# Two gated delta-rule recurrences in a mixed model kernel: the state read through the keys, the transfers of the block inverse merged, and weight loads placed one pair later

## The chip, the cores and the metric

The kernel runs on one core of one Trainium2 chip. The metric is the device time of one execution in microseconds (us). Matrix products run on TensorE (PE in the profile; its weight loads are PEld), elementwise work on VectorE (DVE) and ScalarE (ACT), small serial work on GpSimd (POOL), and SyncE (SP) issues nearly all DMAs. Each engine runs its own instructions in order and the engines meet through semaphores.

## The reference, cut to what matters

The model is three blocks: a gated delta-rule mixer with a mixture of experts (MoE), a state-space mixer with MoE, and a block of an S5 scan, a convolution and sparse attention with a feed-forward layer. The change touches the first mixer alone. For each head, a chunk of the sequence has keys k, queries q, values v, a write strength beta and a cumulative log decay gcum, and a state S of 128x128 is carried from chunk to chunk:

```python
kb = kc * bc[..., None]
lower = jnp.where(strict, jnp.einsum('nbhid,nbhjd->nbhij', kb, kc) * decay, 0.0)
rhs = jnp.concatenate([vc * bc[..., None], kb * jnp.exp(gcum)[..., None]], axis=-1)
sol = lax.linalg.triangular_solve(eye + lower, rhs, left_side=True, lower=True, unit_diagonal=True)
u, w = sol[..., :dv], sol[..., dv:]
...
def step(S, inp):
    v_new = u_i - jnp.einsum('bhck,bhkv->bhcv', w_i, S)
    o = (jnp.einsum('bhck,bhkv->bhcv', q_i * jnp.exp(g_i)[..., None], S)
         + jnp.einsum('bhij,bhjv->bhiv', a_i, v_new))
    S = (S * jnp.exp(g_last)[..., None, None]
         + jnp.einsum('bhck,bhcv->bhkv', k_i * jnp.exp(g_last[..., None] - g_i)[..., None], v_new))
```

With T the inverse of (eye + lower), v_new is T(beta v) - (T(beta exp(gcum) k)) S, and this is also T(beta v - beta exp(gcum) (k S)). The recurrence runs forward and backward over 768 tokens.

## The kernel before, in words

The eight heads are worked in two halves of four heads (`hg` 0 and 1). In each half a projection makes q, k and v, then a recurrence runs, then `gdn_out` makes the output. The recurrence has six pairs (p = 0 to 5, n = 6 hg + p): a pair is one chunk of 128 tokens of the forward direction and one of the backward direction (u = 0 and 1, "units"). One block of work is four heads of one unit: four 128x128x128 products into one bank of PSUM (eight matmul instructions in the trace, two per fp32 product), or one 128x512 instruction on VectorE or ScalarE.

The matrix "lower" of a pair (`rX`) is made two pairs ahead (`decays`, `scores`; the last step counts up `r_xt`). Its inverse begins with its 16x16 diagonal blocks, which take a way through memory:

- SP writes both matrices to `low_in` in HBM (line 887, 2 DMAs of 256 KB, after `r_xt`), waits until they landed, and reads the blocks back with one block to a partition (line 892, 8 DMAs of 8 KB).
- GpSimd inverts all of them (`low_inverse`, lines 993 to 1002), counting up `r_el`.
- SP writes the inverses and their transposes as blocks to `low_u` and `low_t` (line 900, 16 DMAs of 8 KB), waits, and reads the four whole matrices back into `rU` and `rT` (lines 907 and 908, 4 DMAs of 256 KB).
- Only when these landed does the loop go to the next pair. After pair 1 it issues the loads of `EARLY`, six of 1 MB: the weights of the gate and of the output projection and two items of the next stage. In the first pair it issues the loads of `GAP_LATE` between lines 892 and 900.

TensorE's order in a pair is written out by hand: `level_y` (line 1297) waits for the inverted blocks of this pair; then `level_update` (1305, 1306), `decays` and `scores` of pair p + 2, the second level, `last_y` (1317), `last_update` (1329) and between these `turned` (1340, 1341: k and v transposed). Then for both units `weights_w` (1350: T times beta exp(gcum) k, transposed), `values_own` (1357: T times beta v, with a `spread` on line 1260 that broadcasts the decays), `values_state` (1368: minus w S onto the same bank), `output_state` (1376) and `output_own` (1384 the output, 1386 the state's update). Between them stand ScalarE's negated copy of w into `rX` (line 2350, `r_nw`), its Exp of the spread (2353, `r_eb`) and its copy of v_new into `vB` (2356, `r_vnc`). VectorE scales the transposed k into `kB` and v into `vB` (2981 and 2982, `r_kvs`), makes `rY` for the state (2988, `r_yc`), the queries (2994, 2996, `r_q`), and adds to output and state (3002 to 3005, `r_state`) in the next pair.

Of the kernel before, what the change touches and what calls it, by code (L numbers as in the profile page):

```python
# [9 lines left out]
ALU = mybir.AluOpType  # L10
# [363 lines left out]

def build(nc, A):
    with ExitStack() as stack:
# [76 lines left out]
        beg = carve(NT, 16)  # L453
        ea = carve(16)
# [4 lines left out]
        rD, rY, kB, vB, qE = ([carve(HG, P) for _ in range(2)] for _ in range(5))  # L459
# [378 lines left out]
        LOW_DMAS, LOW_BASE = 16 * 30, 16 * 4  # L838

        def blocks_of(name, u, j):  # L840

            whole = A[name][u].rearrange("p j c -> j (p c)" if False else "p j c -> p j c")
            return bass.AP(whole.tensor, whole.offset + j * P, [[LOW * HG * P + LOW, P // LOW], [HG * P, LOW], [1, LOW]])
# [20 lines left out]
        def _(sp):  # L864
# [15 lines left out]
            def low_blocks(hg):  # L880

                for p in range(PAIRS):
                    n = hg * PAIRS + p
                    sp.wait_ge(s.r_low, LOW_DMAS * n + LOW_BASE)
# [8 lines left out]
                    if p == 0:  # L893
                        for item in GAP_LATE[hg]:
                            load(item)
# [5 lines left out]
                    sp.wait_ge(s.r_low, LOW_DMAS * n + 416 + LOW_BASE)  # L901
# [45 lines left out]
        def _(pool):  # L947
# [32 lines left out]
            def low_inverse(n):  # L980
# [4 lines left out]
                if n:  # L985
                    pool.wait_ge(s.r_low, LOW_DMAS * (n - 1) + 416 + LOW_BASE)
# [4 lines left out]
                pool.wait_ge(s.r_low, LOW_DMAS * n + 160 + LOW_BASE)  # L991
# [90 lines left out]
        def _(pe):  # L1082
# [164 lines left out]
            def recurrence(hg):  # L1247
# [96 lines left out]
                def weights_w(p, u):  # L1344

                    n, b, z = hg * PAIRS + p, own(p, u), 2 * (p % 2) + u
                    pe.wait_ge(s.r_kvs, 2 * n + u + 1)
                    pe.wait_ge(s.r_u, 4 * n + 2 + u + 1)
                    for j in range(HG):
                        mm = pe.matmul(ps[:, b, heads[j]], kB[u][:, j, :], rU[z][:, j, :], start=True, stop=True)  # L1350
                    mm.then_inc(s.r_w, 1)

                def values_own(p, u):

                    n, b, z = hg * PAIRS + p, own(p, u), 2 * (p % 2) + u
                    for j in range(HG):
                        pe.matmul(ps[:, b + 1, heads[j]], rU[z][:, j, :], vB[u][:, j, :], start=(j == 0), stop=False)
                    pe.wait_ge(s.r_tbq, n + 1)
                    spread(tbq, u, side(p, u) + 1).then_inc(s.r_in2, 1)

                def values_state(p, u):

                    n, b = hg * PAIRS + p, own(p, u)
                    pe.wait_ge(s.r_nw, 2 * n + u + 1)
                    if p:
                        pe.wait_ge(s.r_state, 2 * (n - 1) + u + 1)
                    for j in range(HG):
                        mm = pe.matmul(ps[:, b + 1, heads[j]], rX[2 * (p % 3) + u][:, j, :], S[u][:, j, :], start=False, stop=(j == HG - 1))
                    mm.then_inc(s.r_vn, 1)
# [33 lines left out]
                for p in range(PAIRS):  # L1403
# [21 lines left out]
                    for u in units:  # L1425
                        weights_w(p, u)
                    for u in units:
                        values_own(p, u)
                    for u in units:
                        values_state(p, u)  # L1430
# [774 lines left out]
        def _(act):  # L2205
# [107 lines left out]
            def recurrence(hg):  # L2313
# [20 lines left out]
                for p in range(PAIRS):  # L2334
# [16 lines left out]
                    for u in units:  # L2351
# [415 lines left out]
        def _(dve):  # L2767
# [80 lines left out]
            def gdn_scalars():  # L2848
# [13 lines left out]
                v.do(dve.tensor_tensor(beg, beg, beta, ALU.mult))  # L2862
# [40 lines left out]
            def recurrence(hg):  # L2903
# [73 lines left out]
                def scaled(p, u):  # L2977
# [3 lines left out]
                    v.do(dve.tensor_tensor(kB[u], g3(side(p, u)), bc(beg[:, tile(p, u), i:i + HG]), ALU.mult))  # L2981
                    v.do(dve.tensor_tensor(vB[u], g3(side(p, u) + 1), bc(beta[:, tile(p, u), i:i + HG]), ALU.mult), s.r_kvs)

# [48 lines left out]
                for p in range(PAIRS):  # L3032
# [31 lines left out]
                    for u in units:  # L3064
                        queries(p, u)
# [794 lines left out]
```

## Time and profile before

| | us |
|---|---|
| median of 3 runs | 4190.58 (4190.25 to 4191.65) |
| the profiled execution | 4194.48 |
| its span in the trace | 4192.4 |
| PE busy | 3823.4 (91%) |
| DVE, ACT, POOL busy | 1825.3, 956.7, 356.4 |
| recurrence of the first half, pairs 0 to 5 | 237.8 to 447.5 |
| recurrence of the second half | 713.6 to 919.8 |
| first waits of PE for the inverted blocks (line 1297), whole span | 27.2, 5 times |

The two recurrences are 416 us, a tenth of the span. How to read it: a busy PE is not yet PE at its peak, so what counts for the recurrences is when each pair begins (its first `level_y`), what PE waited for before it, and which steps lie between two beginnings. PE's granted clock is a share of full speed, 0.50 being 1.2 GHz and 1.00 being 2.4 GHz. In a timeline row, "x16" merges that many neighbouring instructions, and the bracket holds the idle time before them and what ended it.

### The profile page before, as it was taken

The numbers are of one execution on the slowest core, as the hardware profiler recorded it, in microseconds if no ns is written. First come the engines' busy times: TensorE is split into PE (matmuls) and PEld (weight loads), VectorE is DVE, ScalarE is ACT, GpSimd is POOL, SyncE is SP. The second block draws the span as 40 slices with busy tenths as digits, with TensorE's granted clock in tenths as the row PEclk, the third lists the DMA queues.
The fourth block names the chain that finished last, engine by engine and source line by source line (L and its number), as shares of the span: only waits on it lengthen the run. The fifth ranks groups of instructions, "written<-read, shape, count | busy, mean of one in ns | idle before, by whom it ended". The sixth has DMA issues, their size and how long they took to land.

```text
span 4192.4 us, 50922 instructions
## 1 busy us (share of the span) xinstructions
PE 3823.4 (91%) x21420; PEld 2362.6 (56%) x21420; DVE 1825.3 (44%) x2843; ACT 956.7 (23%) x1886; POOL 356.4 (9%) x929
## 2 busy tenths in 40 slices
PE   8989999899999999889998989888888998998999
PEld 4578656875644434677776764222355433446777
DVE  3645445554112212478886540110236467415443
ACT  3421133123211111355654221000124200100000
POOL 0033001210000000000000000000040056100000
PEclk8989999999899999799998999999988999999999
DMA  5232122311498897212101436999921011231331
GB/s 197 86 107 62 51 101 74 112 59 52 176 384 338 340 384 285 73 71 81 61 31 41 126 116 277 421 421 421 341 65 57 26 53 49 75 100 54 108 101 51
DMA packets 278563, 631.30 MB, mean 151 GB/s; under 512 B 63552, under 2 KB 205376, under 8 KB 219456
## 3 DMA queue, kind: packets, MB, share of 16 engines
q1 hardware_dynamic: 275712, 627.40, 40.7%
q8 instruction: 169, 2.77, 0.3%
q10 hardware_dynamic: 2624, 0.66, 0.1%
q14 instruction: 58, 0.48, 0.0%
HBM read 611.75 MB, written 16.25 MB: 150 GB/s over the span
## 4 chain that ended last, share of the span: by engine, by line
PE 68%; DMA 11%; DVE 11%; ACT 3%; issue 3%; SPq 2%; POOL 2%; ACTq 0%; DVEq 0%
PE ps L1867 11%; PE ps L1572 11%; PE ps L1209 6%; PE ps L1918 5%; PE ps L1578 4%; DMA arena<-moe_w_down 4%; DMA arena<-moe_w_gate 2%; PE ps L1479 2%; PE ps L2091 2%; PE ps L1457 2%; PE ps L1725 2%; PE ps L1721 2%; PE ps L1730 2%; DMA arena<-moe_w_up 2%; DVE arena L3453 2%
## 5 line engine op out<-in xcount | busy, mean ns | idle before, releaser
L1572 PE MATMUL ps<-arena 128*64 128x512 f32 x3072 | 709.0, 601 | 79.3 <-DMA arena<-moe_w_up 22.4
L1572 PEld LDWEIGHTS ps<-arena 128*64 128x64 f32 x3072 | 207.6, 137 | 528.9 <-issue 385.7
L3191 DVE SCALAR_TENSOR_TENSOR arena<-arena,ps 128x512 f32<-128x512 f32 (+1 forms) x48 | 30.2, 657 | 525.9 <-PE ps L1572 525.9
L1209 PE MATMUL ps<-arena 128*128 128x512 f32 (+1 forms) x768 | 253.9, 489 | 3.5 <-DVE g_rows L2859 2.1
L1918 PE MATMUL ps<-arena 128*128 128x512 f32 x512 | 229.6, 605 | 5.0 <-DVE arena L3453 4.3
L3453 DVE TENSOR_TENSOR arena<-arena,ps 128x512 f32<-128x512 f32 x86 | 58.4, 687 | 370.8 <-ACT arena L2746 143.5
L1725 PE MATMUL ps<-h_first,w_rest 128*128 128x512 f32 (+1 forms) x576 | 214.5, 388 | 0.5 <-DVE arena L3352 0.5
L1209 PEld LDWEIGHTS ps<-arena 128*128 128x128 f32 x768 | 145.9, 191 | 105.8 <-issue 93.6
L3199 DVE TENSOR_TENSOR m_yx_rest<-ps,m_yx_lead 64x512 fp32r<-64x512 f32 x64 | 44.0, 688 | 362.2 <-ACT m_yc_lead L2460 205.7
L1721 PE MATMUL ps<-h_second,w_rest 128*128 128x512 f32 (+1 forms) x576 | 199.8, 362 | 0.4 <-DVE h_second L3257 0.4
L2460 ACT ACTIVATE m_yx_lead<-ps 64x512 fp32r<-64x512 f32 x64 | 37.9, 592 | 660.7 <-PE ps L1572 660.0
L1578 PE MATMUL ps<-arena 128*32 128x256 f32 x3072 | 175.7, 380 | 0.0
L1918 PEld LDWEIGHTS ps<-arena 128*128 128x128 f32 x512 | 98.9, 195 | 134.4 <-issue 127.1
L1867 PE MATMUL ps<-h_lead,w_lead 128*128 128x512 f32 x352 | 139.6, 397 | 11.4 <-DVE h_rest L3391 6.8
L1578 PEld LDWEIGHTS ps<-arena 128*32 128x32 f32 x3072 | 94.7, 109 | 96.8 <-issue 39.0
L1867 PE MATMUL ps<-h_rest,w_lead 128*128 128x512 f32 x352 | 139.5, 396 | 0.0
L1867 PE MATMUL ps<-h_lead,w_rest 128*128 128x512 f32 x352 | 139.1, 395 | 0.0
L1016 POOL IOTA arena<- 128x64 f32 x2 | 0.4, 186 | 1545.3 <-DVE arena L3431 1410.0
L3453 DVE TENSOR_TENSOR arena<-arena 128x512 f32<-128x512 f32 (+4 forms) x181 | 126.5, 739 | 6.2 <-ACT arena L2697 2.6
L1725 PEld LDWEIGHTS ps<-h_first,w_rest 128*128 128x128 f32 x576 | 112.6, 196 | 20.7 <-issue 3.5
L1730 PE MATMUL ps<-h_first,w_rest 128*128 128x512 f32 (+1 forms) x576 | 124.0, 357 | 0.0
L1721 PEld LDWEIGHTS ps<-h_second,w_rest 128*128 128x128 f32 x576 | 111.5, 194 | 20.1 <-issue 3.1
(499 smaller groups left out, 7060.8 us busy)
## 6 DMA issues: line engine op xcount, KB each, us to landing
arena<-moe_w_gate SPq DMA_DIRECT2D x128, 1024.0 KB, 9.0
arena<-moe_w_up SPq DMA_DIRECT2D x128, 1024.0 KB, 10.2
arena<-moe_w_down SPq DMA_DIRECT2D x128, 1024.0 KB, 11.7
arena<-ada_w SPq DMA_DIRECT2D x48, 1024.0 KB, 4.9
arena<-ffn_w_gate_up SPq DMA_DIRECT2D x22, 1024.0 KB, 5.0
arena<-gdn_w_in SPq DMA_DIRECT2D x16, 1024.0 KB, 9.7
arena<-w_in SPq DMA_DIRECT2D x30, 512.0 KB, 3.8
arena<-ssd_w_x SPq DMA_DIRECT2D x8, 1024.0 KB, 5.1
```

Source lines behind the costliest of these rows:

```text
L1209: mm = pe.matmul(ps[:, 2 * (i % 2) + j, 0:nn], state.w[:, k, m * P:(m + 1) * P], hT[:, k, c0:c0 + nn], start=(k == 0), stop=(k == KD - 1))
L1457: mm = pe.matmul(ps[:, 2 + b + 2 * (j % 2), 0:nn], state.w[:, k, (j % 2) * P:(j % 2) * P + P], hT[:, k, c0:c0 + nn], start=(k == 0), stop= ...
L1479: mm = pe.matmul(ps[:, b + 2 * (m % 2), 0:nn], w[j // 2][:, j % 2, m * P:(m + 1) * P], oT[:, j, c0:c0 + nn], start=(j == 0), stop=(j == HG ...
L1572: mm = pe.matmul(ps[CAPX * h:CAPX * h + CAPX, bank, :], x[:, 0:CAPX], w[:, 512 * h:512 * h + 512], **flags)
L1578: mm = pe.matmul(ps[CAPC * q:CAPC * q + CAPC, bank, 0:CW], x[:, CAPX:SLOTS], w[:, CW * q:CW * q + CW], **flags)
L1721: rests = lambda k: pe.matmul(out, wh[:, k, cols_], hT_lo[k][:, x], start=False, stop=(tail_last and k == KD - 1))
L1725: pe.matmul(out, wh[:, k, cols_], hT_hi[k][:, x], start=(k == 0), stop=False)
L1730: mm = pe.matmul(out, wl[:, k, cols_], hT_hi[k][:, x], start=False, stop=(not tail_last and k == KD - 1))
L1867: mm = pe.matmul(out, a[:, k, cols_], tile_of(b, k), start=(k == 0 and n == 0), stop=(k == tiles - 1 and n == 2))
L1918: mm = pe.matmul(ps[:, bank, :], w[:, k, i * P:(i + 1) * P], h2[:, k, :], start=(k == 0), stop=(k == KD - 1))
L2091: mm = pe.matmul(ps[:, (3 * i + x) % 5, :], w[:, k, (i % 2) * P:(i % 2 + 1) * P], h2[:, k, :], start=(k == 0), stop=(k == KD - 1))
L3453: v.do(dve.tensor_tensor(out, a_, b_, op), sem)
```

## The change

- v_new is made in the other order. `key_states` takes the place of `weights_w`: it multiplies k (not transposed) with S. VectorE's `less_state` takes beta exp(gcum) times that from `vB` (four instructions of 128x128 for each unit, with a column of the new `nbeg` = -beta exp(gcum) as scalar). `values` then applies T once. `values_own`, `values_state`, the scaled keys `kB` and ScalarE's negated copy go. `scaled_last` moves behind `queries`.
- In SP's loop the four DMAs back of pair n no longer wait for their landing before the two of the next matrix are issued (they still do in a half's first and last pair), and `level_y` of the pairs 1 to 4 waits until the next pair's matrix has landed as well (`LOW_AT["matrix", n + 1]`).
- The loads of `EARLY` are issued in pair 2, between its blocks and its inverses, and no longer after the DMAs back of pair 1.

```diff
+LOW_PARTS = {"matrix": 2, "blocks": 8, "inverted": 16, "back": 4}
...
+        LOW_AT, landed = {}, 16 * 4
+        for hg in range(GH // HG):
+            for step in low_order(hg * PAIRS):
+                landed += 16 * LOW_PARTS[step[0]]
+                LOW_AT[step] = landed
...
+                def matrix(n):
                     for u in range(2):
                         sp.wait_ge(s.r_xt, 2 * n + u + 1)
-                        sp.dma_start(A["low_in"][u], rX[2 * (p % 3) + u]).then_inc(s.r_low, 16)
-                    sp.wait_ge(s.r_low, LOW_DMAS * n + 32 + LOW_BASE)
+                        sp.dma_start(A["low_in"][u], rX[2 * ((n - first) % 3) + u]).then_inc(s.r_low, 16)
+                    sp.wait_ge(s.r_low, LOW_AT["matrix", n])
...
-                    if p == 1:
+                    if p == 0 or p == PAIRS - 1:
+                        sp.wait_ge(s.r_low, LOW_AT["back", n])
+
+                for n in range(first, first + PAIRS):
+                    matrix(n)
+                    blocks(n)
+                    if n == first:
+                        for item in GAP_LATE[hg]:
+                            load(item)
+                    if n == first + 2:
                         for item in EARLY[hg]:
                             load(item)
+                    inverted(n)
+                    sp.wait_ge(s.r_low, LOW_AT["inverted", n])
+                    back(n)
...
                     if x == 0:
-                        pe.wait_ge(s.r_low, LOW_DMAS * (n + 1) + LOW_BASE)
+                        pe.wait_ge(s.r_low, LOW_AT["back", n] if p in (0, PAIRS - 1) else LOW_AT["matrix", n + 1])
...
-                def weights_w(p, u):
-
-                    n, b, z = hg * PAIRS + p, own(p, u), 2 * (p % 2) + u
-                    pe.wait_ge(s.r_kvs, 2 * n + u + 1)
+                def key_states(p, u):
+
+                    n, b = hg * PAIRS + p, own(p, u)
                     pe.wait_ge(s.r_u, 4 * n + 2 + u + 1)
...
+                    for j in range(HG):
+                        mm = pe.matmul(ps[:, b + 1, heads[j]], k_[:, j, chunk(p, u)], S[u][:, j, :], start=True, stop=True)
+                    mm.then_inc(s.r_w, 1)
+                    pe.wait_ge(s.r_tbq, n + 1)
+                    pe.wait_ge(s.r_kvs, 2 * n + u + 1)
+                    spread(tbq, u, side(p, u) + 1).then_inc(s.r_in2, 1)
+
+                def values(p, u):
+
+                    n, b, z = hg * PAIRS + p, own(p, u), 2 * (p % 2) + u
+                    pe.wait_ge(s.r_nw, 2 * n + u + 1)
+                    for j in range(HG):
+                        mm = pe.matmul(ps[:, b + 1, heads[j]], rU[z][:, j, :], vB[u][:, j, :], start=True, stop=True)
                     mm.then_inc(s.r_vn, 1)
...
-                        act.wait_ge(s.r_w, 2 * n + u + 1)
-                        a.do(act.activation(flat(rX[2 * (p % 3) + u]), ps[:, own(p, u), :], ACT.Copy, scale=-1.0), s.r_nw)
...
+                def less_state(p, u):
+
+                    n, i = hg * PAIRS + p, 8 * u + hg * HG
+                    dve.wait_ge(s.r_w, 2 * n + u + 1)
+                    for j in range(HG):
+                        v.do(dve.scalar_tensor_tensor(out=vB[u][:, j, :], in0=ps[:, own(p, u) + 1, j * P:(j + 1) * P],
+                                                      scalar=nbeg[:, tile(p, u), i + j:i + j + 1], in1=vB[u][:, j, :], op0=ALU.mult, op1=ALU.add),
+                             s.r_nw if j == HG - 1 else None)
...
                     for u in units:
                         scaled(p, u)
+                    v.settle()
+                    for u in units:
+                        less_state(p, u)
+                    for u in units:
+                        queries(p, u)
                     for u in units:
                         scaled_last(p, u)
-                    for u in units:
-                        queries(p, u)
```

## Rows read from the trace of the kernel before

**Rows 1.** Windows of pairs 1 and 2, first half, and pair 2, second; columns on top.
```profile
core 0: us, PE busy (x) PEld busy (x) DVE busy (x) ACT busy (x) POOL busy (x), PEclk, DMA share, GB/s
277.30:310.60 33.30, 32.30 (x281) 29.45 (x279) 20.33 (x40) 7.54 (x18) 11.02 (x32) 1.00 0.34 111
310.60:355.40 44.80, 34.43 (x279) 31.69 (x279) 20.17 (x40) 7.56 (x18) 11.35 (x36) 0.89 0.26 77
...
782.80:827.30 44.50, 33.66 (x279) 30.89 (x279) 20.20 (x40) 7.55 (x18) 11.35 (x36) 0.88 0.27 78
```

**Rows 2.** PE's timeline, where pairs begin: start, length, line, [idle before <- releaser].
```profile
277.38 1.95 PE L1297 MATMUL ps<-arena 128*128 128x128 f32 x16
...
320.03 3.78 PE L1297 MATMUL ps<-arena 128*128 128x128 f32 x16 [9.38 <-DMA arena<-low_t]
...
388.52 1.95 PE L1297 MATMUL ps<-arena 128*128 128x128 f32 x16
...
417.93 1.95 PE L1297 MATMUL ps<-arena 128*128 128x128 f32 x16
...
749.59 1.95 PE L1297 MATMUL ps<-arena 128*128 128x128 f32 x16
...
792.70 3.47 PE L1297 MATMUL ps<-arena 128*128 128x128 f32 x16 [9.84 <-DMA arena<-low_t]
...
890.25 2.05 PE L1297 MATMUL ps<-arena 128*128 128x128 f32 x16 [0.23 <-DMA arena<-low_t]
```

**Rows 3.** Windows of 1 us, engine PE: window, busy, PEclk, DMA share, GB/s.
```profile
314.00:315.00 1.00, 0.00 (x0) 0.71 0.05 6
...
324.00:325.00 1.00, 1.00 (x8) 0.67 0.25 23
```

**Rows 4.** PE's timeline, second part of pair 1 of the first half.
```profile
297.77 1.06 PE L1350 MATMUL ps<-arena 128*128 128x128 f32 x8
299.32 1.16 PE L1350 MATMUL ps<-arena 128*128 128x128 f32 x8 [0.48 <-DVE arena L2982]
...
303.24 2.05 PE L1368 MATMUL ps<-arena 128*128 128x128 f32 x16
...
309.60 1.06 PE L1386 MATMUL ps<-arena 128*128 128x128 f32 x8
```

**Rows 5.** Groups by shape, DVE and ACT: busy us, mean ns of one, idle before.
```profile
L3222 DVE SCALAR_TENSOR_TENSOR arena<-ps,arena 128x512 f32<-128x512 f32 x64 | 47.8, 746 | 10.8 <-PE ps L1662 10.8
...
L2974 DVE SCALAR_TENSOR_TENSOR arena<-ps,arena 128x256 f32<-128x256 f32 x48 | 22.9, 478 | 0.0
...
L2353 ACT ACTIVATE arena<-ps 128x512 f32<-128x512 f32 x8 | 4.8, 597 | 6.5 <-PE ps L1260 6.5
```

**Rows 6.** SP's timeline, first half: back of pair 1, EARLY, matrix and blocks of pair 2.
```profile
263.86 0.34 SPq L907 DMA_DIRECT2D arena<-low_u  x1
...
265.67 1.36 SPq L878 DMA_DIRECT2D arena<-gdn_w_in  x2
...
274.02 8.10 SPq L887 DMA_DIRECT2D low_in<-arena  x2
288.63 4.20 SPq L892 DMA_DIRECT2D arena<-low_in  x8
```

**Rows 7.** SP's timeline, first half: one whole round, back of pair 3 to pair 4.
```profile
345.99 0.34 SPq L907 DMA_DIRECT2D arena<-low_u  x1
...
352.41 0.80 SPq L887 DMA_DIRECT2D low_in<-arena  x2
355.10 2.85 SPq L892 DMA_DIRECT2D arena<-low_in  x8
371.39 0.26 SPq L900 DMA_DIRECT2D low_u<-arena  x1
...
378.42 0.34 SPq L907 DMA_DIRECT2D arena<-low_u  x1
```

**Rows 8.** SP's timeline, second half: first DMA back of pair 1.
```profile
739.14 0.34 SPq L907 DMA_DIRECT2D arena<-low_u  x1
```

More of the change, by code:

```diff
@@ L371, in __init__, with low_order @@
         self.n, self.uses, self.w = 0, [0] * (RING + DEEP), None
+LOW_PARTS = {"matrix": 2, "blocks": 8, "inverted": 16, "back": 4}
+def low_order(first):
+    return [(kind, n) for n in range(first, first + PAIRS) for kind in ("matrix", "blocks", "inverted", "back")]
 def build(nc, A):
@@ L453, in build @@
         beg = carve(NT, 16)
+        nbeg = carve(NT, 16)
         ea = carve(16)
@@ L458, in build @@
         rT, rU = [carve(HG, P) for _ in range(4)], [carve(HG, P) for _ in range(4)]
-        rD, rY, kB, vB, qE = ([carve(HG, P) for _ in range(2)] for _ in range(5))
+        rD, rY, vB, qE = ([carve(HG, P) for _ in range(2)] for _ in range(4))
         low = [carve(LOW * LOW) for _ in range(4)]
@@ L837, in build @@
         EARLY = [PLAN[PLAN.index(FIRST_OUT[hg]):PLAN.index(RECUR_AT[hg])] for hg in range(GH // HG)]
-        LOW_DMAS, LOW_BASE = 16 * 30, 16 * 4
+        LOW_AT, landed = {}, 16 * 4
[3 more added lines that the diff above has]
+                LOW_AT[step] = landed
         def blocks_of(name, u, j):
-            whole = A[name][u].rearrange("p j c -> j (p c)" if False else "p j c -> p j c")
+            whole = A[name][u]
             return bass.AP(whole.tensor, whole.offset + j * P, [[LOW * HG * P + LOW, P // LOW], [HG * P, LOW], [1, LOW]])
@@ L880, in low_blocks, with blocks @@
             def low_blocks(hg):
-                for p in range(PAIRS):
-                    n = hg * PAIRS + p
-                    sp.wait_ge(s.r_low, LOW_DMAS * n + LOW_BASE)
+                first = hg * PAIRS
+                def matrix(n):
                     for u in range(2):
                         sp.wait_ge(s.r_xt, 2 * n + u + 1)
-                        sp.dma_start(A["low_in"][u], rX[2 * (p % 3) + u]).then_inc(s.r_low, 16)
-                    sp.wait_ge(s.r_low, LOW_DMAS * n + 32 + LOW_BASE)
+                        sp.dma_start(A["low_in"][u], rX[2 * ((n - first) % 3) + u]).then_inc(s.r_low, 16)
+                    sp.wait_ge(s.r_low, LOW_AT["matrix", n])
+                def blocks(n):
                     for u in range(2):
@@ L892, in low_blocks, with inverted @@
                             sp.dma_start((low[0], low[1])[u][32 * u + 8 * j:32 * u + 8 * j + 8, :].rearrange("b (r c) -> b r c", c=LOW), src).then_inc(s.r_low, 16)
-                    if p == 0:
-                        for item in GAP_LATE[hg]:
-                            load(item)
+                def inverted(n):
                     sp.wait_ge(s.r_el, n + 1)
@@ L900, in low_blocks, with back @@
                                 sp.dma_start(blocks_of(name, u, j), low[2 + (x + u) % 2][32 * u + 8 * j:32 * u + 8 * j + 8, :].rearrange("b (r c) -> b r c", c=LOW)).then_inc(s.r_low, 16)
-                    sp.wait_ge(s.r_low, LOW_DMAS * n + 416 + LOW_BASE)
+                def back(n):
+                    p = n - first
                     if p == 0:
@@ L985, in low_inverse @@
                 if n:
[L986 removed]
+                    pool.wait_ge(s.r_low, LOW_AT["inverted", n - 1])
                 g.settle()
@@ L990, in low_inverse @@
                 g.do(pool.affine_select(out=w, in_=w, compare_op=ALU.not_equal, fill=1.0, base=0, pattern=[[1, LOW], [-1, LOW]], channel_multiplier=0))
-                pool.wait_ge(s.r_low, LOW_DMAS * n + 160 + LOW_BASE)
+                pool.wait_ge(s.r_low, LOW_AT["blocks", n])
                 g.settle()
@@ L1342, in turned @@
                     mm.then_inc(s.r_kv, 1)
-                def weights_w(p, u):
-                    n, b, z = hg * PAIRS + p, own(p, u), 2 * (p % 2) + u
-                    pe.wait_ge(s.r_kvs, 2 * n + u + 1)
+                def key_states(p, u):
+                    n, b = hg * PAIRS + p, own(p, u)
                     pe.wait_ge(s.r_u, 4 * n + 2 + u + 1)
[L1349 to L1364, printed above, removed]
                     if p:
                         pe.wait_ge(s.r_state, 2 * (n - 1) + u + 1)
+                    else:
+                        pe.wait_ge(s.r_kvs, 2 * n + u + 1)
                     for j in range(HG):
-                        mm = pe.matmul(ps[:, b + 1, heads[j]], rX[2 * (p % 3) + u][:, j, :], S[u][:, j, :], start=False, stop=(j == HG - 1))
+                        mm = pe.matmul(ps[:, b + 1, heads[j]], k_[:, j, chunk(p, u)], S[u][:, j, :], start=True, stop=True)
+                    mm.then_inc(s.r_w, 1)
+                    pe.wait_ge(s.r_tbq, n + 1)
+                    pe.wait_ge(s.r_kvs, 2 * n + u + 1)
+                    spread(tbq, u, side(p, u) + 1).then_inc(s.r_in2, 1)
[4 more added lines that the diff above has]
+                        mm = pe.matmul(ps[:, b + 1, heads[j]], rU[z][:, j, :], vB[u][:, j, :], start=True, stop=True)
                     mm.then_inc(s.r_vn, 1)
@@ L1425, in recurrence @@
                     for u in units:
-                        weights_w(p, u)
+                        key_states(p, u)
                     for u in units:
-                        values_own(p, u)
-                    for u in units:
-                        values_state(p, u)
+                        values(p, u)
                     for u in units:
@@ L2348, in recurrence @@
                     for u in units:
-                        act.wait_ge(s.r_w, 2 * n + u + 1)
-                        a.do(act.activation(flat(rX[2 * (p % 3) + u]), ps[:, own(p, u), :], ACT.Copy, scale=-1.0), s.r_nw)
-                    for u in units:
                         act.wait_ge(s.r_in2, 2 * n + u + 1)
@@ L2861, in gdn_scalars @@
                 dve.wait_ge(s.tl_act, 2)
-                v.do(dve.tensor_tensor(beg, beg, beta, ALU.mult))
+                v.do(dve.scalar_tensor_tensor(out=nbeg, in0=beg, scalar=-1.0, in1=beta, op0=ALU.mult, op1=ALU.mult))
             def project(hg, first):
@@ L3061, in recurrence @@
                         scaled(p, u)
+                    v.settle()
[3 more added lines that the diff above has]
+                        queries(p, u)
                     for u in units:
                         scaled_last(p, u)
-                    for u in units:
-                        queries(p, u)
                 for u in units:
```

1 line of the change is left out of this document (removed).

## Prediction, made before the changed kernel was run

> **What bounds the kernel now.** I read the page first: PE is busy for 91% of the span, so a change inside the recurrences counts only by what it takes off PE's own row of work or off PE's waits. Then I cut the recurrences into windows from one pair's first `level_y` to the next. The reader is to see in [rows 1] that pair 1 of the first half is PE work nearly from end to end (32.30 of 33.30 us), while pair 2 takes 44.80 us for the same 279 matmuls, at a mean clock of 0.89. PE's timeline says why [rows 2]: before pair 2 it stood for 9.38 us, in the second half for 9.84 us, both times ended by a DMA of `low_t`, the last step of the inverse's way through memory. Pair 1 had no such wait, and the last pair of the second half had 0.23 us. So two things limit a half: PE's own work, 33.1 us in each of the pairs 0 to 3 (277.38 to 310.5 [rows 2, 4]) and 29.4 us in the last two (388.52 to 417.93 [rows 2]), and a round of SP, DMA and GpSimd that takes 32.4 us a pair (345.99 to 378.42 [rows 7]). They are nearly even: the 0.23 us is the proof. The forecast therefore follows both through the pairs.
>
> **The 9.4 us wait.** In pair 1, SP issued the DMAs back at 263.86, the six loads of `EARLY` from 265.67, and then the next matrix at 274.02. That issue took 8.10 us, and the matrix had landed only at 288.63 [rows 6]. Loads and matrix, 6.5 MB, thus kept the DMA engines for 23.0 us. An undisturbed round has 9.1 us from the first DMA back to the first block read (345.99 to 355.10 [rows 7]); here it was 24.8 us. The change issues the matrix right after the DMAs back and puts the loads behind the block reads, where GpSimd works anyway.
>
> What it takes away beside the idle time is a slow start: the clock fell from 1.00 to 0.50 within the window 314 to 315, some 4 us after PE had stopped, and came back within 324 to 325, PE having worked from 320.03 [rows 2, 3]. Pair 2 took 44.8 - 9.4 = 35.4 us of its own against 33.1, so 2.3 us in the first half. In the second, 44.5 - 9.8 - 33.1 = 1.6 us [rows 1, 2]. Sum of wait and clock: 11.7 and 11.4 us.
>
> **PE's own work.** From 303.24 to 309.60 PE ran seven blocks, 0.91 us each; the pair ends one block later, at 310.5 [rows 4]. Before, the part from `weights_w` on has twelve blocks and two spreads: 310.5 - 297.77 = 12.7 us. After, ten blocks and the same spreads: two blocks less, 1.8 us. The second `weights_w` also began 1.55 us after the first, 0.64 us more than a block, since it waited for VectorE's scaling of k and v of unit 1 [rows 4]. `key_states` needs neither; its spread does need `vB`, but VectorE then scales one tile instead of two for each unit and is done a whole instruction earlier. So 0.6 us go too. Together 2.4 us a pair, and 14.4 a half.
>
> What must be hidden for that is the new link key_states, `less_state`, `values`. The trace has no 128x128 instruction of that kind. A 512-wide one takes 746 ns, a 256-wide one 478 [rows 5]: by the slope 344 ns for 128 columns. Four cost between 1.07 us (starts 0.27 apart, if they overlap as the slope suggests) and 1.4 us (one after the other). I take 1.15. With key_states(0) at 0: it ends at 0.9, VectorE takes off the state until 2.2, PE meanwhile does spread(0), key_states(1) and spread(1) until 2.9 to 3.0, and values(0) finds its tile. Unit 1: key_states ends about 2.5, VectorE until 3.7, values(1) would start at 3.8: just in time. Then VectorE does both queries, 0.9 us each, until 4.6 and 5.5 (ScalarE's Exp takes 0.60 [rows 5] and begins right after each spread), and PE's output_state wants them at 4.7 and 5.6. `scaled_last` comes after, until 6.1 and 6.7; output_own wants it at 6.5 and 7.4. Margins of 0.1 to 0.4 us: no stall at 1.15 us, about 0.3 us a pair at 1.4. ScalarE loses two copies of 0.60 us a pair, off the path: worth nothing. VectorE trades two scalings for eight short instructions, with 13 of 33 us idle in the pair [rows 1]. Moving `scaled_last` behind the queries is costed at nothing, its cover being output_state; without it, up to 0.6 us a pair.
>
> VectorE's short instructions pay a fixed part: from the two widths, 0.21 of the 0.344 us [rows 5]. The Trainium skill speaks against such splitting (VectorE: DVE Perf Modes, The TRN2 errata: "many small tiles pay it per-tile", tiles of at least 512 are advised). By its table for a PSUM source, 120 cycles plus one per column at 0.96 GHz, four would be an estimated 1.03 us and the margins above would hold.
>
> **The round through memory.** Now SP's own rhythm. From the first DMA back to the first block read it took 6.4 us (1 MB back) plus 2.7 us (the matrix); then 16.3 us to the first inverse written (block reads, GpSimd), then 7.0 us to the next DMAs back: 32.4 us [rows 7]. After, six DMAs of 256 KB stand in the queue together. The 9.1 us can become 6.4 at best (the matrix hidden in the way back) and 9.1 at worst (they only share the bandwidth). I take 7.2, nearer to the low end, since waiting for a landing has a part in which nothing moves; the round is then 30.5 us, between 29.7 and 32.4.
>
> But PE now waits for matrix and back in the pairs 1 to 4, not for back alone. Followed through the first half: back of pair 1 is issued at 263.86, all six have landed at 271.1, block reads are issued until 273.9, then the 6 MB of loads, which at the pace above occupy the queue for 21 us, until 295. The inverses of pair 2 are ready at 271.1 + 16.3 = 287.4 and would be through at 294.4, but they stand behind the loads: 296. Then landed and ready for PE: 303.2, 333.7, 364.2 for the pairs 2 to 4, and for the last pair, which waits for back alone, 387.5 + 6.4 = 393.9. PE would come to them at 305.7 (275.0 plus 30.7), 336.4, 367.1 and 394.1. So PE never waits, by 0.2 to 2.9 us, and the half ends 26.1 us earlier (11.7 + 14.4). Pair 0's wait stays, as its order is untouched.
>
> In the second half the way back of pair 1 starts at 739.14 for a pair that begins at 749.59, 10.45 us, against 13.52 in the first half [rows 2, 6, 8]: 3.1 us less in hand. There the pairs 2 to 4 are even to within 0.6 us and the last pair waits some 2.9 us: 11.4 + 14.4 - 2.9 = 22.9 us.
>
> **Sum.** 26.1 + 22.9 = 49.0 us. Everything after a recurrence starts from its last matmul (`gdn_out`'s loads have long landed even one pair later: pair 3 begins near 336, they are wanted near 421), so it moves as a whole. The profiled execution would go from 4194.5 to 4145.5. It stands 3.9 us above the median of the runs, 4190.58, and I set the forecast against the median: 4141.5 us. Ends of the unknown prices: with a round of 29.7 us nothing waits, 52 us gained, and with 0.3 us more a pair from VectorE's side 4138; a PE gain of 2.7 instead of 2.4 us a pair, which the round then mostly eats, 4136.
>
> **Rivals.**
> 1. *The round sets the pace.* If the six DMAs only share the bandwidth (9.1 us, a round of 32.4 us), the last pairs wait 7.5 us in the first half and 10.6 in the second, and each wait beyond some 4 us costs about 2 us of clock [rows 3]. Gain 52 - 18 - 4 = 30 us, 4160. A smaller form: the sixteen small writes of pair 2 can't even be issued while the loads fill the queue, as the matrix's two took 8.10 us [rows 6]. Then they go out after 295, the DMAs back follow at about 302 instead of 296, and both halves lose some 6 us: 37 us, 4153. For it: the 8.10 us, and the evenness of round and PE. Against it: the 13.4 us from the last block read's issue to the first inverse (357.95 to 371.39 [rows 7]) cover more than half of the loads. The Trainium skill says the same of the queue (DMA: Bandwidth & Descriptors, Queues, rings and completion order): descriptors on each engine are taken in ring order. The landing at 288.63 agrees, and no sum here needs the sentence.
> 2. *VectorE's link stalls PE.* If the short instructions cost so much, with the semaphores between, that PE loses what the two blocks gave, only waits and clock are won: 23 us, 4167. For it: margins of 0.1 us at three places. Against: the slope of [rows 5].
> 3. *Slower than before.* The same link, but so long that it eats everything: from key_states(1) to the last `scaled_last` VectorE is now one serial queue on which values, output_state and output_own of both units hang. It decides from 2.4 + 23/12 = 4.3 us of stall a pair. If each 128-wide instruction cost the full 746 ns, the link would be 3 us longer than planned, still 1.3 short of it; at 5 us a pair, the kernel would take about 4199. Nothing in the rows has that price.
> 4. *It does not do what it says.* The wait before pair 2 is moved, not removed: PE's new wait for matrix n + 1 is late by as much, because `r_xt` comes late. But that matrix is ready two pairs ahead. Gain then 12 times 2.4 less what the round eats, 15 to 20 us: 4173.
>
> **Chances.** Forecast, 4135 to 4148: 0.60. Rival 1 with both forms, 4148 to 4161: 0.22. Rival 2: 0.08. Rival 4: 0.03. Rival 3: 0.03. Within 0.2% (8.4 us, about what a measurement of this kernel can tell from no change): 0.02. The rest, 0.02, for more gain than 56 us. The range of 4134 to 4160 takes in the forecast and rival 1. Faster by over 0.2%: 0.95; within: 0.02; slower: 0.03.
>
> **What would show it.** In the changed kernel: no idle time before pair 2's `level_y` and a clock of 1.00 from pair 1 on; pair lengths on PE of 30.7 and 27.0 us; in SP's timeline about 7.2 us from the first DMA back to the first block read; the first inverse of pair 2 written near 287 and its DMAs back near 296; PE idle on VectorE before `values`, `output_state` and `output_own` of at most 0.3 us a pair in all; a short wait for a DMA before the last pair of the second half. The forecast is wrong if the pairs are longer than 31.5 us with PE waiting for VectorE (rival 2), or if waits for DMAs stand before several of the pairs 2 to 5 (rival 1), or if what follows the recurrences does not move with them.

## The result and the profile after

| | before | after |
|---|---|---|
| median, us | 4191.11 (4 runs) | 4153.77 (4151.91 to 4156.37, 4 runs) |
| span of the profiled execution | 4192.4 | 4153.3 |
| recurrence of the first half, first `level_y` to last matmul | 209.6 | 190.7 |
| recurrence of the second half | 206.2 | 185.9 |

The ratio is 0.9909, with a 95% interval from 0.9895 to 0.9923: 37 us faster, where 49 were forecast. The two recurrences are 39.1 us shorter, and so is the span: all of the gain lies in them. Since the rest of the program varies by some microseconds from run to run, the recurrences' lengths in the trace are the finer instrument below. They have a limit of their own, told under the experiments.

Where pairs begin in the changed kernel, on PE's timeline (start, length, line, in brackets the idle time before and its releaser; `level_y` is now line 1326):

```profile
274.07 1.95 PE L1326 MATMUL ps<-arena 128*128 128x128 f32 x16
...
305.10 2.05 PE L1326 MATMUL ps<-arena 128*128 128x128 f32 x16 [0.28 <-DMA low_in<-arena]
...
337.28 2.05 PE L1326 MATMUL ps<-arena 128*128 128x128 f32 x16 [1.24 <-DMA low_in<-arena]
...
369.02 2.05 PE L1326 MATMUL ps<-arena 128*128 128x128 f32 x16 [0.64 <-DMA low_in<-arena]
...
399.07 3.68 PE L1326 MATMUL ps<-arena 128*128 128x128 f32 x16 [2.81 <-DMA arena<-low_t]
...
761.60 2.05 PE L1326 MATMUL ps<-arena 128*128 128x128 f32 x16 [1.59 <-DMA low_in<-arena]
...
852.95 3.65 PE L1326 MATMUL ps<-arena 128*128 128x128 f32 x16 [2.94 <-DMA arena<-low_t]
```

They answer to [rows 2]. The two waits of 9.4 and 9.8 us are gone, but waits on a DMA now stand before six of the eight pairs 2 to 5, where before, beside pair 2, only one of 0.2 us stood. `low_in` as releaser is the new thing: PE waits for the next pair's matrix. The last pair of each half begins slowly (3.68 us for sixteen matmuls that take 1.95). Windows on engine PE show that this is the clock (window, its length, busy time and count, PEclk, DMA share, GB/s):

```profile
398.00:399.00 1.00, 0.00 (x0) 1.00 0.04 14
399.00:401.00 2.00, 1.93 (x9) 0.54 0.00 0
401.00:402.00 1.00, 1.00 (x7) 0.50 0.00 0
402.00:403.00 1.00, 1.00 (x8) 0.72 0.00 0
403.00:404.00 1.00, 1.00 (x11) 1.00 0.00 0
```

After the wait of 2.81 us the granted clock was near 0.50 for some 3 us.

The second part of pair 1 on PE, to be laid beside [rows 4] (1382 `key_states`, 1393 `values`, 1401 `output_state`, 1411 the state's update):

```profile
294.47 1.05 PE L1382 MATMUL ps<-arena 128*128 128x128 f32 x8
...
295.87 1.16 PE L1382 MATMUL ps<-arena 128*128 128x128 f32 x8
...
297.38 2.05 PE L1393 MATMUL ps<-arena 128*128 128x128 f32 x16
299.27 1.98 PE L1401 MATMUL ps<-arena 128*128 128x128 f32 x16
...
303.77 1.06 PE L1411 MATMUL ps<-arena 128*128 128x128 f32 x8
```

No bracket stands in it: PE waits for nothing there. From `key_states` to the pair's end at 304.66 (its last block's start plus 0.9 us, as in the prediction) it takes 10.2 us, where it took 12.7. VectorE's side of the same stretch, and its new instruction in the view by shape:

```profile
295.63 1.13 DVE L3008 SCALAR_TENSOR_TENSOR arena<-ps,arena 128x128 f32<-128x128 f32 x4 [0.27 <-PE ps L1382]
297.07 1.13 DVE L3008 SCALAR_TENSOR_TENSOR arena<-ps,arena 128x128 f32<-128x128 f32 x4 [0.31 <-PE ps L1382]
298.11 0.16 DVE L3022 COPY arena<-arena 128x4 f32<-128x4 f32 x1
298.31 0.84 DVE L3024 TENSOR_TENSOR arena<-arena 128x512 f32<-128x512 f32 x1
```
```profile
L3008 DVE SCALAR_TENSOR_TENSOR arena<-ps,arena 128x128 f32<-128x128 f32 x96 | 27.1, 344 | 6.9 <-PE ps L1382 6.9
```

Four of them take 1.13 us, one 344 ns. Lines 3022 and 3024 are the queries, which begin as soon as unit 1 is done.

SP's timeline of the first half, to be laid beside [rows 6] and [rows 7] (901 matrix, 908 block reads, 891 the loads, 915 inverses, 924 the way back):

```profile
262.71 0.34 SPq L924 DMA_DIRECT2D arena<-low_u  x1
...
264.52 0.91 SPq L901 DMA_DIRECT2D low_in<-arena  x2
270.88 2.84 SPq L908 DMA_DIRECT2D arena<-low_in  x8
273.76 1.91 SPq L891 DMA_DIRECT2D arena<-gdn_w_in  x2
275.72 1.35 SPq L891 DMA_DIRECT2D arena<-gdn_w_out  x2
277.12 7.54 SPq L891 DMA_DIRECT2D arena<-gdn_w_in  x2
287.49 0.42 SPq L915 DMA_DIRECT2D low_u<-arena  x1
...
288.70 0.71 SPq L915 DMA_DIRECT2D low_u<-arena  x1
...
293.54 0.32 SPq L915 DMA_DIRECT2D low_u<-arena  x1
...
296.13 0.33 SPq L915 DMA_DIRECT2D low_t<-arena  x1
297.65 0.35 SPq L924 DMA_DIRECT2D arena<-low_u  x1
...
305.08 4.13 SPq L908 DMA_DIRECT2D arena<-low_in  x8
322.48 0.26 SPq L915 DMA_DIRECT2D low_u<-arena  x1
...
329.52 0.34 SPq L924 DMA_DIRECT2D arena<-low_u  x1
```

The matrix of pair 2 now goes out at 264.52 and has landed at 270.88; before it was 288.63. The loads sit behind its block reads. From the first inverse written to the first DMA back it takes 10.2 us in pair 2 (287.49 to 297.65), against 7.0 in pair 3 (322.48 to 329.52). The difference lies in SP's issues: the first eight of the sixteen writes go out over 6.05 us (287.49 to 293.54), some 0.75 us apart, the others 0.37 us apart as in pair 3, and from the last write's issue to the first DMA back it is 1.5 us in both pairs. So the loads ahead hold up the issuing of the small writes. A round, first DMA back to first DMA back, is 31.9 us here (297.65 to 329.52).

### The profile page after: what moved, and what is told of

It reads as the page before. It is cut to its first block, busy times and chain, and to the rows that moved or that the text cites. A ratio compares the mean times of both kernels' runs of the same rounds, so it can differ in the third digit from the quotient of the medians.

```text
span 4153.3 us, 50594 instructions
## 1 busy us (share of the span) xinstructions
PE 3793.5 (91%) x21228; PEld 2334.8 (56%) x21228; DVE 1836.4 (44%) x2915; ACT 942.2 (23%) x1862; POOL 356.8 (9%) x929
## 4 chain that ended last, share of the span: by engine, by line
PE 66%; DMA 11%; DVE 11%; ACT 3%; POOL 3%; issue 3%; SPq 3%; ACTq 0%; DVEq 0%
PE ps L1595 11%; PE ps L1890 11%; PE ps L1238 6%; PE ps L1941 5%; PE ps L1601 4%; DMA arena<-moe_w_down 4%; DMA arena<-moe_w_gate 2%; PE ps L1502 2%; PE ps L2114 2%; PE ps L1480 2%; PE ps L1748 2%; PE ps L1744 2%; PE ps L1753 2%; DMA arena<-moe_w_up 2%; DVE arena L3484 2%
## 6 DMA issues: line engine op xcount, KB each, us to landing
arena<-moe_w_up SPq DMA_DIRECT2D x128, 1024.0 KB, 10.2
```

## The experiments

The table collects them. Each ratio is against the kernel before on the same chip; "recurrences" is the sum of both halves in the profiled execution, and "pair 0" the part of it from the first `level_y` to the end of pair 0, in both halves together.

| kernel | ratio to before (95%) | recurrences, us | of these, pair 0 |
|---|---|---|---|
| before | 1 | 415.7 | 75.6 |
| after | 0.9909 (0.9895 to 0.9923) | 376.6 | 70.8 |
| x1_early_back | 0.9983 (0.9974 to 0.9992) | 401.8 | 72.8 |
| x2_no_merge | 0.9932 (0.9911 to 0.9952) | 386.8 | 69.7 |
| x3_algebra_only | 1.0011 (1.0000 to 1.0022) | 421.1 | 70.3 |
| x8_algebra_exact | 1.0008 (0.9997 to 1.0020) | 414.5 | 74.2 |
| x4_transfers_only | 0.9950 (0.9930 to 0.9969) | 391.7 | 75.3 |
| x5_spread | 0.9904 (0.9885 to 0.9923) | 376.7 | 71.0 |
| x6_own_semaphore | 0.9913 (0.9897 to 0.9930) | 379.8 | 72.9 |
| x7_half_writes | 0.9870 (0.9855 to 0.9885) | 358.7 | 66.5 |
| x9_half_and_spread | 0.9846 (0.9829 to 0.9862) | 357.4 | 66.5 |
| x10_old_algebra_half | 0.9932 (0.9916 to 0.9949) | 389.6 | 71.6 |

Each length comes from one execution. Pair 0 begins after a wait for DMAs, at a granted clock that differs from trace to trace, and its length follows that clock: with the new algebra 33.7 us in the changed kernel's second half (mean clock 0.94), 35.8 us in the first half of x6_own_semaphore (0.87), 37.2 us in the changed kernel's first half (0.84). So two kernels can differ by some 3 us a half in pair 0 without the edit having a part in it, and where it matters pairs 1 to 5 are given apart. The whole times agree with the lengths on what is large: by the ratios x1 is 31 us slower than the changed kernel, x2 10 and x4 17, by the lengths 25, 10 and 15.

The theory from the profile after: PE's own work is now shorter than the round through SP, DMA and GpSimd, and the round sets when the later pairs begin. The rival: PE's own work still sets the end, and the missing gain is elsewhere.

**The new algebra alone.** The first try kept SP's loop of the changed kernel with its pieces put back (and PE waits for `LOW_AT["back", n]` in every pair):

```diff
-                    if p == 0 or p == PAIRS - 1:
-                        sp.wait_ge(s.r_low, LOW_AT["back", n])
+                    sp.wait_ge(s.r_low, LOW_AT["back", n])
...
                     back(n)
+                    if n == first + 1:
+                        for item in EARLY[hg]:
+                            load(item)
```

> The state read through the keys and the inverse applied once, with SP's order and waits as in the kernel before. Theory (the round sets the end): PE saves 2.5 us a pair on its own work, but the wait before pair 2 grows from 9.4 to about 14 us, and the last pairs begin when their DMAs land. Gain 5 to 10 us, 4181 to 4186. Rival (PE's work is the bound): gain 12 x 2.5 = 30 us, 4161.

It came out 5.4 us longer in the recurrences, not 5 to 10 us shorter. Part of that is the edit: here the loads stand behind the wait for the landing, where the kernel before has them ahead of it, so that they and the matrix of pair 2 go out later (first load in the second half 5.75 us after the first DMA back, against 1.8 us; first block read of pair 2 28.5 and 27.2 us after it, against 24.8 and 24.0). So the same was done with SP's loop copied from the kernel before:

> The state read through the keys and the inverse applied once, with SP's loop and all its waits word for word those of the kernel before (the loads right behind the DMAs back, ahead of the wait for their landing). Theory (the round sets the end): PE's own work falls by 2.5 us a pair, the wait before pair 2 grows by 5 us to about 14.5, the last pair waits 4 to 6 us; recurrences 3 to 8 us shorter than before, 4183 to 4188. Rival (PE's own work is the bound): 25 to 30 us shorter.

PE's timeline of this kernel, pair 2 and the last pair of the first half (`level_y` is line 1306):

```profile
319.68 3.78 PE L1306 MATMUL ps<-arena 128*128 128x128 f32 x16 [13.81 <-DMA arena<-low_t]
...
415.70 3.78 PE L1306 MATMUL ps<-arena 128*128 128x128 f32 x16 [4.67 <-DMA arena<-low_t]
```

Pair 2 begins at 319.68, in the kernel before at 320.03 [rows 2]: PE was ready 4.8 us earlier and waited 4.4 us more. The recurrences are 1.2 us shorter, under the 3 to 8 expected, and the time can't be told from before; pairs 1 to 5 take 340.4 us, in the kernel before 340.1, so in them nothing is gained. PE's pair 1 takes 30.6 us, as in the changed kernel, so PE does save 2.5 us a pair, and all of it behind pair 0 goes into waits (of 13.8, 0.3 and 4.7 us in the first half) and the slow clock after them. The rival, 25 to 30 us, is out.

**The transfers alone.** TensorE, VectorE and ScalarE as before, with the changed kernel's `low_blocks`, `LOW_AT` and waits. Against the changed kernel it reads, in short:

```diff
-                        key_states(p, u)
+                        weights_w(p, u)
                     for u in units:
-                        values(p, u)
+                        values_own(p, u)
+                    for u in units:
+                        values_state(p, u)
```

> SP's new order (matrix with the way back, loads one pair later) with TensorE, VectorE and ScalarE as in the kernel before. Theory: pair 2's wait of 9.4 and 9.8 us and the slow clock after it (2.3 and 1.6 us) go, PE's pairs stay 33.1 and 29.4 us, longer than the round, so hardly a wait is left: gain 20 to 24 us, 4167 to 4171. The two halves of the change then sum to about 30 us where both together gave 37. Rival (the wait moves on to later pairs): gain under 12 us.

The recurrences are 24.0 us shorter (20 to 24 were expected; the median of 4172.5 lies 1.5 us beyond 4167 to 4171), and no pair behind pair 0 waits for anything. Pair 2 (`level_y` is line 1325):

```profile
311.26 1.95 PE L1325 MATMUL ps<-arena 128*128 128x128 f32 x16
```

So the transfers alone give 24.0, the algebra alone 1.2, both 39.1 us: together 13.9 more than their sum. The algebra's 30 us of PE work can be collected only as far as the round allows.

**The place of the loads.**

```diff
-                    if n == first + 2:
-                        for item in EARLY[hg]:
-                            load(item)
                     inverted(n)
                     sp.wait_ge(s.r_low, LOW_AT["inverted", n])
                     back(n)
+                    if n == first + 1:
+                        for item in EARLY[hg]:
+                            load(item)
```

> The changed kernel, but with the six weight loads issued again right after the DMAs back of pair 1, ahead of the matrix of pair 2. Theory (waits and round set the end, PE's own work is covered by them): the matrix lands near 288 us, so the wait before pair 2 is back at 10 to 14 us and the clock falls again; after it the round through memory (31.5 us) is longer than PE's 30.6 us, so nothing is caught up. Gain over the kernel before 7 to 13 us, 4178 to 4184. Rival (the loads' place hardly matters, PE's shorter work carries the gain): within 5 us of the changed kernel, about 4155.

The recurrences are 25.2 us longer than in the changed kernel: the loads' place is the largest part of the change. The time, 4184.9, lies just beyond the 4178 to 4184 expected. The wait is back, but before pair 1 and not before pair 2, since in this kernel pair 1 waits for the matrix of pair 2:

```profile
289.88 3.78 PE L1326 MATMUL ps<-arena 128*128 128x128 f32 x16 [14.89 <-DMA low_in<-arena]
```

**The matrix with the way back.** The change to SP is the first hunk of x3; PE waits for `LOW_AT["back", n]` in every pair.

> The changed kernel, but SP waits for the four DMAs back of every pair before it issues the next matrix, and PE waits for back alone. Theory A (six DMAs together save about 1.2 us a round over 9.1 us, and the round sets the end): the last pairs of both halves begin 2 to 4 us later than in the changed kernel, while the waits of 0.3 to 1.6 us before the pairs 2 to 4 mostly go: 3 to 8 us slower than the changed kernel, 4157 to 4162. Theory B (merging gives nothing, since PE must now wait for the matrix too): same as or faster than the changed kernel, 4150 to 4155.

Theory A held, at more than its upper end: 10.2 us longer. Six rounds average 32.3 us, against 31.4 in the changed kernel, and the last pairs wait 5.8 and 4.3 us. What did not come is that the waits before the pairs 2 to 4 mostly go: one of 3.0 us stands in the first half, 1.4, 0.2 and 2.1 us in the second. Each wait over 2 us also begins its pair at a lower clock.

**PE's wait for both.** The matrix's DMAs count on a semaphore of their own:

```diff
-                        pe.wait_ge(s.r_low, LOW_AT["back", n] if p in (0, PAIRS - 1) else LOW_AT["matrix", n + 1])
+                        pe.wait_ge(s.r_low, LOW_AT["back", n])
```

> The changed kernel, but the matrix DMAs count on a semaphore of their own, and PE waits in every pair for back alone, not for the next matrix too. Theory (the round sets the end): the waits of 0.3 to 1.6 us before the pairs 2 to 4 go, and the wait before the last pair grows by as much; the recurrences keep their length within 2 us. Rival (PE's wait for both DMAs is what costs): recurrences 4 to 5 us shorter, with the last pair's wait unchanged at 3 us.

PE's timeline, pairs 4 and 5 of the first half:

```profile
365.06 2.05 PE L1327 MATMUL ps<-arena 128*128 128x128 f32 x16 [1.40 <-DMA arena<-low_t]
...
396.82 3.78 PE L1327 MATMUL ps<-arena 128*128 128x128 f32 x16 [4.57 <-DMA arena<-low_t]
```

The waits of the middle pairs went for the most part to the last pair, as the theory says. The sum is 3.2 us longer than in the changed kernel, more than the 2 us allowed, but 2.1 of them lie in pair 0, which the edit does not touch; pairs 1 to 5 are 1.1 us longer. The rival wanted 4 to 5 us less and is out. The `low_in` brackets of the changed kernel named a wait that cost nothing of its own that these traces can tell.

**The loads spread.**

```diff
-                    if n == first + 2:
-                        for item in EARLY[hg]:
+                    if 2 <= n - first < 5:
+                        for item in EARLY[hg][2 * (n - first) - 4:2 * (n - first) - 2]:
                             load(item)
```

> The changed kernel with the six weight loads spread, two in each of the pairs 2, 3 and 4, at the same place between block reads and inverses. Theory (the loads delay pair 2's small writes by 3 us, and this delay stands before every later pair, as the round is the slower of the two): pair 2's DMAs back go out 7.0 us after the first inverse instead of 10, the waits before the pairs 2 to 5 fall from 5.6 and 4.9 us a half to 2 to 3 us, and the slow clock of the last pair goes. Recurrences 5 to 9 us shorter than in the changed kernel. Rival (two loads a pair delay each pair's small transfers a little): no shorter.

This missed: 376.7 us, no shorter than 376.6. The first step came as expected, pair 2's DMAs back follow its first inverse by 7.0 us and no longer by 10.2. But the six DMAs behind them then took 7.8, 8.9 and 9.7 us from the first DMA back to the first block read in the first half, and 8.7, 7.8 and 7.6 in the second, against 6.8 to 7.7 in the changed kernel from pair 2 on. Whether this comes from two loads a pair or is the scatter of such DMAs is not settled. Scatter of that size needs no spread loads: with all six in pair 2, x6 has a value of 9.0 us and x10_old_algebra_half one of 9.5.

**A shorter round.** In the last kernels the inverse and its transpose lie interleaved, on chip and in HBM, and one DMA takes both:

```diff
-                            for x, name in enumerate(("low_u", "low_t")):
-                                sp.dma_start(blocks_of(name, u, j), low[2 + (x + u) % 2][32 * u + 8 * j:32 * u + 8 * j + 8, :].rearrange("b (r c) -> b r c", c=LOW)).then_inc(s.r_low, 16)
+                            sp.dma_start(blocks_of("low_ut", u, j), low_both[32 * u + 8 * j:32 * u + 8 * j + 8, :].rearrange("b (r c) -> b r c", c=LOW)).then_inc(s.r_low, 16)
...
-                a, raw, w, wt = (block(x, both) for x in low)
+                a, raw = (block(x, both) for x in low)
+                w, wt = (low_both[both, :].rearrange("p (r s c) -> p r s c", s=2, c=LOW)[:, :, x, :] for x in range(2))
```

> The changed kernel with the sixteen writes of inverted blocks made eight: the inverse and its transpose lie interleaved on chip and in HBM, so one DMA of 16 KB takes both. SP's issue of them takes 3 us instead of 5.9. Theory (the round sets the end): a round falls from 31.4 to 28.5 us, under PE's 30.6; all waits from pair 3 on go, and with them the slow clock of the last pair; recurrences 9 to 13 us shorter than in the changed kernel. Rival (PE or the loads set the end): under 3 us.

SP's timeline, one round, and windows of pair 2 and of the last pair of the first half (window, its length, busy time and count of PE, PEld, DVE, ACT, POOL, then PEclk, DMA share, GB/s):

```profile
342.55 3.15 SPq L917 DMA_DIRECT2D low_ut<-arena  x8
347.25 0.34 SPq L926 DMA_DIRECT2D arena<-low_ut  x1
...
349.06 0.90 SPq L904 DMA_DIRECT2D low_in<-arena  x2
354.43 2.85 SPq L911 DMA_DIRECT2D arena<-low_in  x8
371.29 3.14 SPq L917 DMA_DIRECT2D low_ut<-arena  x8
376.05 0.34 SPq L926 DMA_DIRECT2D arena<-low_ut  x1
```
```profile
297.70:328.30 30.60, 30.01 (x264) 27.51 (x263) 21.11 (x46) 6.35 (x16) 10.49 (x34) 1.00 0.24 60
...
385.90:412.70 26.80, 24.69 (x228) 23.13 (x227) 16.32 (x37) 3.90 (x8) 0.00 (x0) 1.00 0.00 1
```

From the first inverse to the first DMA back it takes 4.7 us, the round 28.8 us (347.25 to 376.05; 28.9 on average), and PE's pairs stand back to back at full clock: one wait of 0.5 us is left behind pair 0. The recurrences are 17.9 us shorter than in the changed kernel, more than the 9 to 13 expected: 13.6 us in pairs 1 to 5 and 4.3 in pair 0. The wait before pair 0 is no part of the recurrences, but with earlier DMAs back it is 1.4 and 1.7 us where it was 4.1 and 4.4, and the mean clock of pair 0 is 0.90 and 1.00 where it was 0.84 and 0.94. That the shorter wait made the clock is likely (x9 has the same waits and the same 66.5 us), but no run tests it by itself. The kernel is 1.3% faster than the one before.

**The bound after that.** Two kernels ask whether PE is now the limit. The first is x7 with the edit of x5, the second x4 with the edit of x7.

> Eight writes of 16 KB instead of sixteen of 8 KB, and the six weight loads spread over the pairs 2 to 4. With eight writes alone one wait was left, 0.7 us before pair 2 of the second half, and in neither half did the last pairs wait. Theory (PE's own work is now the bound): recurrences as long as with eight writes alone, 358 to 360 us, within 3 us. Rival (spreading helps further): 3 us or more shorter.

> TensorE, VectorE and ScalarE as in the kernel before, with SP's new order and eight writes of 16 KB. Theory (the kernel before's work on PE, 33.1 us a pair, is longer than the round with sixteen writes already): shortening the round gives only what pair 0 gains by its earlier DMAs back, about 6 us; recurrences 385 to 390 us against 391.7 with sixteen writes and against 358.7 with the new algebra, so that the new algebra is worth its full 12 x 2.5 = 30 us once the round is short, where it was worth 15 us with sixteen writes. Rival (the new algebra's gain is capped elsewhere): recurrences within 20 us of 358.7.

Both came as the theory has them. With the loads spread as well, 357.4 us, within 3 us of 358.7 (its whole time is the lowest measured, 4127 against 4192 on its chip, but 19 us of its span against x7's lie outside the recurrences and are no effect of this edit that the trace shows). With the old algebra and the short round, 389.6 us. So the new algebra is worth 1.2 us with SP's old loop, 15.1 with the changed one (391.7 to 376.6) and 30.9 with the short round (389.6 to 358.7), and that last is its 12 x 2.54 us of PE work in full. In pairs 1 to 5 alone the three are 0, 10.6 and 25.8 us.

## Why the prediction came out as it did

The sign was right, and so was the account of what the change removes; the size was 12 us too large. The measured 4153.8 lies in the range of 4134 to 4160, but not in the forecast itself (4135 to 4148, chance 0.60): it lies in the interval of rival 1 (4148 to 4161, 0.22), and rival 1's sign, waits for DMAs before several of the pairs 2 to 5, came up. So the range held because it took in rival 1, and the round is the slower chain, as that rival has it. That the rival's smaller form names the very number, 37 us and 4153, is luck: it put some 6 us a half on pair 2's small writes alone, and the shortfall has three sources. By its steps:

- *The 9.4 us wait goes, and the slow clock with it.* Right: 0.28 and 1.59 us of idle time before pair 2, and its own length is 30.8 us. x1 shows that it was the loads' place.
- *PE's own work falls by 2.4 us a pair.* Right: pair 1 takes 30.6 us (274.07 to 304.66), 2.5 less; pair 4 takes 27.1 (369.02 to 396.09) where 27.0 was said.
- *VectorE's link hides.* Right, and the slope between two widths gave the price exactly: 344 ns, four in 1.13 us (taken: 1.15). The lower bound of 1.07 was a slip: it counts four spacings of 0.27 us, where three spacings and the last instruction's 0.344 make 1.15; and no row shows the 0.27, which this trace puts at 0.26. No idle time of PE on VectorE in this part. The Trainium skill's warning against short instructions (VectorE: DVE Perf Modes, The TRN2 errata) is true of their price, 0.21 of 0.344 us fixed, and the 1.03 us that the prediction worked out from its table for four was 0.10 low; but they lie in a stretch where PE had other work. Rivals 2 and 3 had no part in it.
- *The way through memory becomes 30.5 us a round.* This term was mis-sized: rounds took 31.9, 31.9 and 31.4 us in the first half, 30.3, 30.4 and 32.7 in the second, 31.4 on average. The six DMAs together were taken well (7.2 us said, 7.35 on average from pair 2 on). The rest of the round, 23.3 us, was taken from one round [rows 7], and that was one of the shortest: the six undisturbed rounds of the kernel before average 23.8, those of the changed one 24.1.
- *The loads delay pair 2 by some 1.6 us.* Under-sized: 3.1 us in the first half (10.2 against 7.0) and 2.5 in the second (9.5 against 7.0). In the same round the six DMAs took 8.2 and 7.9 us, not 7.2. This is the smaller form of rival 1 with its mechanism, writes that can't be issued, at less than half of its price (302 where 294.4 was undisturbed, 7.6 us), and with it every later pair starts later.
- *No waits in the first half, 2.9 us in the second.* Wrong by these two: 5.6 and 4.9 us, 7.6 us more than forecast. (They are counted from where the next matmul would have started, which is 0.16 us more for each wait than its bracket.)
- *Only a wait beyond some 4 us costs clock.* Wrong: the last pairs waited 2.8 and 2.9 us and ran their first matmuls at half clock, 1.5 and 1.7 us each, 3.2 us that the forecast did not have. The 4 us were read from one fall [rows 3]; of the waits behind pair 0 in these runs, those up to 1.8 us left the clock alone and those from 2.1 us on did not. That is no rule for other places: before pair 0 of x7's first half, a wait of 0.48 us that ended at 229.98 and one of 1.40 us that ended at 232.40 were followed by a granted clock of 0.50 (235 to 240).

Sum: 49.0 - 7.6 - 3.2 + 12 x 0.14 (PE's own) = 39.9 against the 39.1 measured; the 0.8 us between them stay open. Rival 4 is out too: the matrix of the next pair was always ready to go when SP came to it. The working was careful about which chain is longer, pair by pair, and saw that they were nearly even; it then took the single observed round as typical, and where two chains are even, each 0.9 us of a round that comes three times a half moves the last pair by as much.

## What to carry to other kernels

When two chains take turns at 31 and 33 us, shortening one alone gives what the other leaves: measure both against each other before choosing, and price the partner first (the algebra here was worth 1, 15 or 31 us by the length of the round and the place of the loads). A wait moved from one releaser to another (`low_in` in the middle pairs) is no cause; the question is which chain the last wait hangs on. Where many small DMAs are issued one by one in such a chain, their count is the first thing to cut: eight fewer took 2.5 us off each round and 17.9 us off the recurrences, nearly half of what the whole change gave (13.6 of them behind pair 0). And before a sum over stages is compared with another, look whether a stage that the edit leaves alone has moved: pair 0 moved by up to 3.5 us a half.

## What the runs showed that was not expected

- Waits of PE of 2.1 to 2.9 us already cost clock. Sixteen matmuls that take 1.95 us took 3.68 after a wait of 2.81 us, 3.30 after 2.08 us (x2, second half), and 2.05 after 1.59 us. What is lost does not grow evenly with the wait: after 3.02 us (x2, first half) they took 2.67.
- Equal DMAs scatter: the six DMAs of a round took between 6.8 and 7.7 us from pair 2 on in the changed kernel, and up to 9.0 in x6, 9.5 in x10 and 9.7 in x5.
- The small writes are paid at SP, not on the DMA engines: sixteen of 8 KB took 7.0 us to the next step, eight of 16 KB with the same bytes 4.7. Of these, 5.5 and 2.8 us lie between the first issue and the last, 1.5 and 1.9 behind the last.
- Loads issued ahead hold up SP itself: 14 us after the first of six 1 MB loads the small writes still went out 0.75 us apart in place of 0.37, for eight of them.
